# A hybrid decoder layer on one core: output weights loaded in the sixth tile, q's weights in two halves, a router that reads h, and a moved output projection

## The chip, the cores and the metric

The kernel runs on one core of a Trainium2 chip. The metric is the device time of one execution in microseconds (us), lower is better; several runs are taken and their median is compared. A core has five engines that run their own instruction streams and wait for each other on semaphores: TensorE (PE, matrix products and turns, that is transposes), VectorE (DVE), ScalarE (ACT), GpSimd (POOL), and SyncE (SP), which here only issues DMAs. All arithmetic is float32.

## What is computed

One step of a decoder layer, for a prompt of 1024 tokens (eight tiles of 128) and eight sample tokens, each with its own cache and state. The width is 1024. Cut to what matters:

```python
xn = rms_norm(x, norm1)
q, k, v, z, xbc, dt = split(xn @ w_in)
attn = sliding_window_attention(rope(norm(q)), rope(norm(k)), v, sinks)   # window 128
ssm, new_conv, new_h = ssd_mixer(z, xbc, dt, ...)     # conv of 4 taps, chunked scan, gate, norm
h = x + concat(attn, ssm) @ w_out
t = rms_norm(h, norm2)
g = softmax(t @ w_grp + b_grp);  e = t @ w_exp + b_exp        # 4 groups of 8 experts
y = h + sum over the top 2 experts of the best group: gate * (silu(t @ w_gate) * (t @ w_up)) @ w_down
```

The outputs are y for prompt and sample, and the new caches, convolution rows and states.

## The kernel before, in words

**Start.** SP issues, in this order (L364 to L396): the first tile's token rows `x`, the same rows by channel `x_chan` (a view of `mix_back`), the rope table, `norm1`, all constants `con`, the weights of q (2 MB), of k and v, of dt, eleven small parameters, two halves of xBC's weights, z's weights, the second tile's rows, and then everything that only the output stage needs: `w_out` (4 MB), `norm2`, the router's weights `w_route` and biases `b_route`. ACT squares x, POOL makes the reciprocal root, PE spreads it over the partitions (L1679), DVE scales `x_chan` into `xT` (L989). PE then projects q, k/v (`project`, L1584), xBC (`pe_xbc`, L1628) and z.

**Tile loop.** `pe_tile`, `dve_tile`, `act_tile` and `pool_tile` handle tile n and, in PE's gaps, project tile n+1. PE's order in a tile: scores (L1715), q of the next tile, products of B and C and turns (L1722, L1724), k/v and part of xBC of the next tile, turns of the probabilities (L1732), the decay product of the scan (L1737, which waits for the matrix `m`), L1739, the attention values (L1745), the state product (L1750), the rest of xBC, the turn of y (L1759, waits for the normed y), keys, z. `m` needs the cumulative sums of the tile copied to all partitions: SP writes them to memory and reads them back (`move_cum`, L405 to L410), POOL subtracts and clips (L1457, L1460), ACT exponentiates, DVE multiplies (L1067). SP's order in a tile is: rows of a later tile, `move_cum`, the spill of the mixed tile `mix` to memory (`spill`, L398).

**Output stage.** Nine turns `i`, in the order tiles 0 to 6, sample, tile 7 (`ORDER`). PE in each turn: half of the output projection (`pe_out(i, 0)`, L1644, 16 matmul records), the turn of the previous tile's t (`pe_turn_t`, L1580), the rank product of the one before (`pe_rank`), a piece of the sample's work, the other half (`pe_out(i, 1)`), the previous tile's router product (`pe_router`, L1664), more of the sample's work. A product with eight rows (`pe_state`, L1825) spreads B and C of one sample token over the partitions; ACT empties its two banks by turns (L749, L750). DVE adds the residual (`dve_residual`, L901, signal `hres`), ACT stores h and squares it, POOL makes the root (signal `hs`), DVE writes t (`dve_norm2`, L909, signal `td`), ACT stores t, PE turns it (signal `ttm`), ACT copies the turned tile to `tT`, PE multiplies with `w_route`, and DVE chooses the experts in some 20 short operations (`dve_router`, L912; `dve_rank`, `dve_choices`). `back(i)` is the buffer of x that becomes h; SP fills it and `mix_back` for turn i once turn i-2 is through (`load_next_back`, L448).

**Experts.** When the table of slots is made (`slot_table`, L1306), POOL copies the first indices (L1511), gathers rows of t (L1514) and PE runs through 32 slots of one expert each with 128 rows, whose weights SP loads four ahead; results are scattered to `y_dram`. At the end DVE adds two rows per token to h (L1407) for tiles 0 to 7 and then the sample (L1403), and ACT stores y (L840).

```python
def now(eng, names, tile):       # waits until the signal has come for this tile
    eng.wait_ge(S[name], tile + (CREDIT + 1))
def last(eng, names, tile):      # ... for the tile before
    eng.wait_ge(S[name], tile + CREDIT)
```

## Time and profile before

| | |
|---|---|
| median of 3 runs | 876.75 us (875.34 to 882.05) |
| the profiled execution | 883.72 us, of which the span of the core's instructions is 881.9 us |
| PE busy / its weight loads | 770.5 us (87%) / 548.1 us (62%) |
| DVE, ACT, POOL busy | 474.7 us (54%), 271.0 us (31%), 226.4 us (26%) |
| mean granted clock of TensorE | 0.926 of full speed |
| DMA | 140.49 MB, mean 159 GB/s |

The profile is of one execution. A row of the timeline gives the start, the duration, the engine (PEld is PE's weight load; SPq, ACTq and POOLq are queues of issues), the line, the operation, what it writes and reads, and in brackets how long the engine stood before it and what ended that. The chain of waits follows the work that ended last back to the start. The stages in the timeline: start to 53 us, tile loop to 406, output stage to 622, experts to 840, last sums to the end.

### The profile page before, as it was taken

What the parts mean: (1) busy time and instruction counts of PE and PEld (TensorE: products, weight loads), DVE (VectorE), ACT (ScalarE), POOL (GpSimd) and SP (SyncE); (2) the same over time, 40 slices, a digit from 0 to 9 for tenths busy, and PEclk for the clock granted to TensorE, in tenths of its full rate; (3) what the DMA queues carried; (4) which work ended last, traced back from release to release, by engine and by line L of the source; (5) the groups of instructions that cost most, each with busy time, mean ns of one, the idle gap of its engine ahead of it and who ended that gap; (6) DMA issues with size and microseconds to landing.
All of it is one profiled execution on the core that took longest, in us unless ns stands there. A gap on an engine that the chain in (4) does not pass through costs nothing.

```text
span 881.9 us, 12933 instructions
## 1 busy us (share of the span) xinstructions
PE 770.5 (87%) x4328; PEld 548.1 (62%) x4328; DVE 474.7 (54%) x1224; ACT 271.0 (31%) x662; POOL 226.4 (26%) x270
## 2 busy tenths in 40 slices
PE   4977999999999999986999999895799999999900
PEld 1845777776777777742564455344688877778800
DVE  1555879797979797974245443545222222222246
ACT  1342363635353636452132221201122222222200
POOL 0024233333333333230001100300334333333200
PEclk9987999999999999997998898996699999999965
DMA  7980202020202010135644551504699988886178
GB/s 257 340 223 32 98 1 86 14 98 0 97 0 96 0 51 0 48 104 177 212 169 146 188 195 67 203 3 144 218 324 331 332 308 309 296 299 250 67 263 324
DMA packets 64364, 140.49 MB, mean 159 GB/s; under 512 B 18068, under 2 KB 30132, under 8 KB 64300
## 3 DMA queue, kind: packets, MB, share of 16 engines
q1 hardware_dynamic: 51604, 110.39, 37.0%
q0 software_dynamic: 9216, 16.93, 5.2%
q10 hardware_dynamic: 3504, 12.68, 3.6%
q8 instruction: 20, 0.33, 0.2%
q14 instruction: 20, 0.16, 0.1%
HBM read 120.37 MB, written 37.34 MB: 179 GB/s over the span
## 4 chain that ended last, share of the span: by engine, by line
PE 37%; issue 20%; DMA 15%; DVE 12%; POOL 5%; POOLq 4%; DVEq 4%; ACT 2%; SPq 1%; ACTq 0%
PE bank L1644 14%; DMA w_arena<-in_w_down 9%; PE bank L1936 8%; DVE cv L1006 6%; PE bank L1942 4%; PE bank L1580 3%; DMA w_arena<-y_dram 3%; POOLq L1459 2%; PE bank L1588 2%; POOL rstd L1418 2%; DVEq L873 2%; PE bank L1628 2%; POOLq L1417 2%; POOL cv L1460 1%; DMA w_arena<-in_w_in 1%
## 5 line engine op out<-in xcount | busy, mean ns | idle before, releaser
L1644 PE MATMUL bank<-w_out_sb,mix_back 128*128 128x512 f32 x256 | 128.9, 663 | 7.0 <-issue 5.2
L1936 PEld LDWEIGHTS bank<-w_arena 128*128 128x128 f32 x992 | 116.8, 196 | 27.4 <-issue 23.2
L1936 PE MATMUL bank<-w_arena 128*128 128x128 f32 x992 | 119.8, 280 | 7.7 <-DMA w_arena<-in_w_down 6.8
L1644 PEld LDWEIGHTS bank<-w_out_sb,mix_back 128*128 128x128 f32 x256 | 53.0, 212 | 75.1 <-issue 75.0
L1588 PE MATMUL bank<-w_arena,tT 128*128 128x512 f32 (+1 forms) x192 | 73.0, 535 | 3.8 <-DMA w_arena<-in_w_in 3.8
L1588 PE MATMUL bank<-w_arena,xT 128*128 128x512 f32 (+1 forms) x192 | 72.0, 528 | 0.0
L1353 DVE TENSOR_TENSOR w_arena<-w_arena,bank 128x128 f32<-128x128 f32 x32 | 9.2, 288 | 115.0 <-ACT w_arena L805 115.0
L1006 DVE SCALAR_TENSOR_TENSOR cv<-raw,conv_w_sb,cv 128x128 f32<-128x128 f32 x192 | 65.1, 400 | 4.6 <-ACT cv L630 2.3
L1416 POOL TENSOR_TENSOR stat<-stat,eps 128x1 f32<-128x1 f32 (+4 forms) x35 | 9.1, 259 | 206.1 <-ACT junk L651 115.1
L1942 PE MATMUL bank<-w_arena 128*128 128x512 f32 x124 | 60.4, 609 | 0.7 <-DVE w_arena L1353 0.7
L1628 PEld LDWEIGHTS bank<-tT,w_arena 128*128 128x128 f32 x512 | 58.1, 192 | 1.2 <-DMA w_arena<-in_w_in 0.5
L1628 PEld LDWEIGHTS bank<-xT,w_arena 128*128 128x128 f32 x512 | 58.4, 192 | 0.5
L1628 PE MATMUL bank<-tT,w_arena 128*128 128x128 f32 x512 | 58.5, 276 | 0.1
L1628 PE MATMUL bank<-xT,w_arena 128*128 128x128 f32 x512 | 58.5, 275 | 0.0
L1588 PEld LDWEIGHTS bank<-w_arena,tT 128*128 128x128 f32 x192 | 36.3, 194 | 35.1 <-issue 33.3
L1588 PEld LDWEIGHTS bank<-w_arena,xT 128*128 128x128 f32 x192 | 35.8, 191 | 30.4 <-issue 28.6
L901 DVE TENSOR_TENSOR x<-x,bank 128x512 f32<-128x512 f32 (+1 forms) x18 | 12.4, 686 | 71.6 <-PE bank L1644 57.2
L1359 DVE COPY s<-bank 128x512 f32<-128x512 f32 x32 | 22.1, 692 | 37.0 <-PE bank L1942 37.0
L805 ACT ACTIVATE w_arena<-bank 128x128 f32<-128x128 f32 x32 | 8.9, 277 | 107.0 <-PE bank L1936 107.0
L702 ACT ACTIVATE s<-s,top 128x256 f32<-128x256 f32 x64 | 31.6, 494 | 27.9 <-DVE top L1049 27.9
L1518 POOL DMA_INDIRECT y_dram<-s,idx_out x32 | 32.5, 1015 | 24.1 <-issue 22.4
L1418 POOL TENSOR_TENSOR rstd<-stat,neg_half 128x1 f32<-128x1 f32 (+4 forms) x35 | 36.0, 1029 | 5.3 <-issue 0.6
(310 smaller groups left out, 1247.0 us busy)
## 6 DMA issues: line engine op xcount, KB each, us to landing
w_arena<-in_w_gate SPq DMA_DIRECT2D x31, 512.0 KB, 4.7
w_arena<-in_w_up SPq DMA_DIRECT2D x31, 512.0 KB, 6.2
w_arena<-in_w_down SPq DMA_DIRECT2D x31, 512.0 KB, 18.4
x<-in_x_prompt SPq DMA_DIRECT2D x16, 512.0 KB, 5.5
w_arena<-in_w_in SPq DMA_DIRECT2D x4, 2048.0 KB, 11.5
w_arena<-y_dram SPq DMA_DIRECT2D x16, 512.0 KB, 10.9
mix_back<-in_x_prompt_by_channel SPq DMA_DIRECT2D x8, 512.0 KB, 4.1
cum_rows<-cum_dram SPq DMA_DIRECT2D x8, 512.0 KB, 4.4
```

The costliest lines, as they stand in the source:

```text
L702: act.activation(s[:, hh, :], s[:, hh, :], ACT.Exp, bias=top[:, 1, hh:hh + 1], accum_out=top[:, 2, hh:hh + 1])
L873: dve.drain()
L1006: dve.scalar_tensor_tensor(out=cv[:, c, :], in0=raw[:, c, k:k + P], scalar=conv_w[:, c, k:k + 1], in1=cv[:, c, :], op0=ALU.mult, op1=ALU.add)
L1359: dve.tensor_copy(yo[u][:, 512:D], bank[7][:, :]).then_inc(E_["yd"], 1)
L1418: pool.tensor_tensor(rstd[0:n, col:col + count], stat[0:n, col:col + count], neg_half[0:n, 0:count], ALU.pow).then_inc(S[done], 1)
L1518: pool.indirect_dma_start(y_dram, bass.IndirectOffsetOnAxis(ap=idx[:, :].bitcast(U32), axis=0), out, None, bounds_check=CHOICES - 1, oob_i ...
L1580: ins = pe.transpose(bank[banks[k // 4]][:, (k % 4) * n:(k % 4 + 1) * n], cols, ids)
L1588: ins = pe.matmul(out, xT[u][:, k, 0:n], w_in[:, k, cols], start=k == 0, stop=k == KC - 1)
L1628: ins = pe.matmul(bank[half][:, c * P:(c + 1) * P], w_in[:, k, at:at + P], xT[u][:, k, :], start=k == 0, stop=k == KC - 1)
L1644: ins = pe.matmul(bank[4 - c][:, :], mix_back[u][:, k, :], w_out[:, k, 512 * c:512 * c + 512], start=k == 0, stop=k == KC - 1)
L1936: ins = pe.matmul(out[:, a * P:(a + 1) * P], gu[:, a, k, :], xgT[w % 2][:, k, :], start=k == 0, stop=k == KC - 1)
L1942: ins = pe.matmul(bank[6 + c][:, :], hidT[w % 2], down[:, 512 * c:512 * c + 512], start=True, stop=True)
```

## The change

The order of the loads at the start: x, the first 128 columns of `con`, `norm1` and `x_chan`, then q's weights in two halves by rows (signals `w_q` and `late_in`; PE waits for the second half only ahead of the fifth of eight steps), then rope and the rest of `con` (signal `w_z`). The output weights, `norm2` and the router's weights and biases are issued, in the same lines, behind the spill of tile 4, in the sixth tile. `norm2` is also loaded by channel and multiplied into `w_route` once; PE turns h instead of t, and DVE scales the router's product by the root `rstd` (two columns, 13 and 14, by turns) as it adds the bias. `load_next_back` waits for `ttm` too, since h is read longer. The first half projection of turn 0 moves into the last tile, ahead of the turn of y. The first of the two state products of turns 3, 4 and 5 moves behind the router. In the last turn the sample's router goes ahead of the second half, ACT copies the turned tile before it stores t, and DVE writes t behind the choices. The first gather takes its indices straight from the slot table. The last sums begin with the sample (`SUMS`).

```diff
+        SUMS = (TILES, *range(TILES))
@@ sync
-            token_rows(0, slice(0, P), slice(0, 1))
+            sp.sem_inc(x_in[0], 16)
+            sp.dma_start(x[0][:, :], flat_x[0:P, :]).then_inc(first_in, 16)
+            sp.dma_start(con[:, 0:P], I["constants"][:, 0:P]).then_inc(first_in, 16)
             sp.dma_start(norm1[:, :], I["norm1"].rearrange("a (p k) -> (a p) k", k=KC)).then_inc(first_in, 16)
-            sp.dma_start(con[:, :], I["constants"]).then_inc(first_in, 16)
-            weights(0, 0, Q_END, w_q)
+            sp.dma_start(x_chan[0][:, :, :], I["x_prompt_by_channel"][0]).then_inc(x_in[0], 16)
+            for half in range(2):
+                kk = slice(half * KC // 2, (half + 1) * KC // 2)
+                sp.dma_start(w_in[:, kk, 0:Q_END], w_rows[:, kk, 0:Q_END]).then_inc((w_q, late_in)[half], 16)
+            sp.dma_start(rope[0][:, :], I["rope"][0:P, :]).then_inc(x_in[0], 16)
+            sp.dma_start(con[:, P:C_END], I["constants"][:, P:C_END]).then_inc(w_z, 16)
...
             token_rows(1, slice(P, 2 * P), slice(1, 2))
-            for kv in range(NKV):
-                load(w_out[kv * HD:(kv + 1) * HD, 0:REP, :],
-                     I["w_out"][0, kv * REP * HD:(kv + 1) * REP * HD].rearrange("(r d) n -> d r n", d=HD))
-            load(w_out[:, REP:KC, :], I["w_out"][0, NH * HD:].rearrange("(c p) n -> p c n", p=P))
-            load(norm2[:, :], row("norm2", P))
-            load(w_route[:, :, 0:NG], I["w_grp"].rearrange("a (p k) n -> (a p) k n", k=KC))
-            load(w_route[:, :, NG:NG + NE], I["w_exp"].rearrange("a (p k) n -> (a p) k n", k=KC))
-            load(b_route[:, 0:NG], row("b_grp", P))
-            load(b_route[:, NG:NG + NE], row("b_exp", P))
...
             spill(4, mix_dram[4])
...
+            load(norm2_chan[:, :], I["norm2"].rearrange("a (p k) -> (a p) k", k=KC))
             rows_free(6)
...
             def load_next_back(i):
-                now(sp, "wob td", i - 2)
+                now(sp, "wob td ttm", i - 2)
...
@@ scalar
             for i in range(2, TILES + 1):
+                if i == TILES:
+                    act_router(act, TILES - 1, DEC)
                 act_residual(act, i)
+                if i == TILES:
+                    act_turned_t(act, i, width(ORDER[i]))
                 act_store_t(act, i)
-                act_router(act, i - 1, width(ORDER[i - 1]))
+                if i < TILES:
+                    act_router(act, i - 1, P)
...
@@ vector
         def dve_router(dve, tile, n, slot):
...
-            dve.tensor_tensor(lg[0:n, 0:NG], bank[7][0:n, 0:NG], b_route[0:n, 0:NG], ALU.add)
-            dve.tensor_tensor(lg[0:n, 8:8 + NE], bank[7][0:n, NG:NG + NE], b_route[0:n, NG:NG + NE], ALU.add)
+            now(dve, "hs", tile)
+            scale = rstd[0:n, 13 + tile % 2:14 + tile % 2]
+            dve.scalar_tensor_tensor(out=lg[0:n, 0:NG], in0=bank[7][0:n, 0:NG], scalar=scale, in1=b_route[0:n, 0:NG], op0=ALU.mult, op1=ALU.add)
+            dve.scalar_tensor_tensor(out=lg[0:n, 8:8 + NE], in0=bank[7][0:n, NG:NG + NE], scalar=scale, in1=b_route[0:n, NG:NG + NE],
+                                     op0=ALU.mult, op1=ALU.add)
...
             dve.wait_ge(loaded, n_loaded[0])
+            dve.tensor_tensor(w_route[:, :, :], w_route[:, :, :], norm2_chan[:, :].unsqueeze(2).to_broadcast([P, KC, NG + NE]), ALU.mult)
...
+                if i == TILES:
+                    dve_router(dve, TILES - 1, DEC, slot_of(TILES - 1))
                 dve_residual(dve, i, 1)
...
-                dve_norm2(dve, i)
+                if i < TILES:
+                    dve_norm2(dve, i)
...
             dve_choices(slice(EARLY, PAIRS), row_sel[2])
+            dve_norm2(dve, TILES)
             dve_router(dve, TILES, P, slot_of(TILES))
...
@@ gpsimd
                 last(pool, "td", tile)
-                root_mean(pool, 13, 1, n, "hs")
+                if tile >= 2:
+                    now(pool, "sel", tile - 2)
+                root_mean(pool, 13 + tile % 2, 1, n, "hs")
...
-            fetch_index(idx_in[0], 0, 0)
-            pool.drain()
-            gather(xg[0], idx_in[0], e_x[0])
+            gather(xg[0], slot_tab[:, 0, 0:1], e_x[0])
@@ tensor
-            pe_q(pe, 0, 0, P, ((w_q, 16),))
+            pe_q(pe, 0, 0, P, ((0, w_q, 16), (KC // 2, late_in, 16)))
...
                     pe_keys(nxt)
+                if n_next == DEC:
+                    pe.wait_ge(loaded, n_loaded[0])
+                    now(pe, "at", tile)
+                    pe_out(pe, 0, 0)
                 now(pe, "yg", tile)
...
         def pe_turn_t(pe, tile, n):
-            now(pe, "td", tile)
+            now(pe, "hres", tile)
             last(pe, "tt", tile)
-            pe_turn_x(pe, t[0:n, :], ident[0:n, 0:n], n, (5, 6), S["ttm"])
+            pe_turn_x(pe, back(tile)[0:n, :], ident[0:n, 0:n], n, (5, 6), S["ttm"])
```

What this makes of PE's order is shown at three places. The rows are PE's instructions in program order, with the line of the kernel they belong to (of after in the second piece; its lines are shifted), the output and inputs, the width and the number of them. `bank` is an accumulator, `con` the constants, here the identity of a turn.

The end of the tile loop and the beginning of the output stage, before:

```order
L1745 MATMUL bank<-pT,v 64x512 x4
L1750 MATMUL bank<-xde,btok 128x256 x2
L1759 MATMUL bank<-con,y 128x128 x4
L1644 MATMUL bank<-w_out_sb,mix_back 128x512 x16
L1776 MATMUL bank<-con,cum_rows 128x8 x8
```

and after:

```order
L1770 MATMUL bank<-pT,v 64x512 x4
L1775 MATMUL bank<-xde,btok 128x256 x2
L1669 MATMUL bank<-w_out_sb,mix_back 128x512 x8
L1788 MATMUL bank<-con,y 128x128 x4
L1669 MATMUL bank<-w_out_sb,mix_back 128x512 x8
L1805 MATMUL bank<-con,cum_rows 128x8 x8
```

Half of the first projection has moved ahead of the turn of y.

Turn 4 of the output stage, from its first half projection to the last piece of the sample's work, before:

```order
L1644 MATMUL bank<-w_out_sb,mix_back 128x512 x8
L1580 MATMUL bank<-con,t 128x128 x8
L1669 MATMUL bank<-both,con 128x32
L1670 MATMUL bank<-counted,con 128x32
L1825 MATMUL bank<-qT,con 128x512
L1644 MATMUL bank<-w_out_sb,mix_back 128x512 x8
L1664 MATMUL bank<-w_route,tT 128x36 x8
L1825 MATMUL bank<-qT,con 128x512
L1837 MATMUL bank<-ps_T,pT 128x8 x8
```

and after:

```order
L1669 MATMUL bank<-w_out_sb,mix_back 128x512 x8
L1604 MATMUL bank<-con,x 128x128 x8
L1694 MATMUL bank<-both,con 128x32
L1695 MATMUL bank<-counted,con 128x32
L1669 MATMUL bank<-w_out_sb,mix_back 128x512 x8
L1689 MATMUL bank<-w_route,tT 128x36 x8
L1854 MATMUL bank<-qT,con 128x512 x2
L1866 MATMUL bank<-ps_T,pT 128x8 x8
```

The state product that stood between the halves now stands with the other one behind the router, and what is turned is x, the buffer that holds h.

The last turn, from the choices on, before:

```order
L1856 MATMUL bank<-raw,s 128x32 x8
L1644 MATMUL bank<-w_out_sb,mix_back 128x512 x8
L1664 MATMUL bank<-w_route,tT 8x36 x8
L1580 MATMUL bank<-con,t 128x128 x8
L1669 MATMUL bank<-both,con 8x32
L1670 MATMUL bank<-counted,con 8x32
L1664 MATMUL bank<-w_route,tT 128x36 x8
```

and after:

```order
L1885 MATMUL bank<-raw,s 128x32 x8
L1689 MATMUL bank<-w_route,tT 8x36 x8
L1669 MATMUL bank<-w_out_sb,mix_back 128x512 x8
L1694 MATMUL bank<-both,con 8x32
L1695 MATMUL bank<-counted,con 8x32
L1604 MATMUL bank<-con,x 128x128 x8
L1689 MATMUL bank<-w_route,tT 128x36 x8
```

The sample's router went ahead of the half projection, and its rank ahead of the turn of h.

## Rows read from the trace of the kernel before

**Rows 1.** The page, its chain of waits: share of the span by engine.
```profile
PE 37%; issue 20%; DMA 15%; DVE 12%; POOL 5%; POOLq 4%; DVEq 4%; ACT 2%; SPq 1%; ACTq 0%
```
**Rows 2.** Timeline, start, PE and its weight loads (start, duration, engine, operation, wait).
```profile
13.66 12.27 PE L1588 MATMUL bank<-w_arena,tT 128*128 128x512 f32 x32 [3.84 <-DMA w_arena<-in_w_in]
25.98 14.37 PEld L1628 LDWEIGHTS bank<-tT,w_arena 128*128 128x128 f32 x128 [0.46 <-DMA w_arena<-in_w_in]
```
**Rows 3.** Timeline, first tile, SP's issues: output weights, and then the cumulative sums.
```profile
29.26 4.09 SPq L350 DMA_DIRECT2D w_out_sb<-in_w_out  x3
...
38.19 16.66 SPq L350 DMA_DIRECT2D w_route<-in_w_exp  x1
...
59.95 0.94 SPq L350 DMA_DIRECT2D b_route<-in_b_exp  x1
...
67.54 0.33 SPq L410 DMA_DIRECT2D cum_rows<-cum_dram  x1
```
**Rows 4.** Timeline, first tile: POOL's and PE's waits, and PE's next xBC.
```profile
71.07 2.44 POOL L1457 TENSOR_TENSOR cv<-cum_rows,cum 128x1024 f32<-128x1024 f32 x1 [15.45 <-DMA cum_rows<-cum_dram]
...
79.71 3.68 PE L1737 MATMUL bank<-xdt,cv 128*128 128x64 f32 x16 [5.18 <-DVE cv L1067]
...
89.67 10.88 PE L1628 MATMUL bank<-xT,w_arena 128*128 128x128 f32 x96
```
**Rows 5.** Timeline, third tile, the same two operations of PE.
```profile
171.58 1.90 PE L1737 MATMUL bank<-xdt,cv 128*128 128x64 f32 x16
...
177.16 10.88 PE L1628 MATMUL bank<-xT,w_arena 128*128 128x128 f32 x96
```
**Rows 6.** Timeline, sixth tile, two issues of SP that follow each other.
```profile
282.14 0.34 SPq L400 DMA_DIRECT2D mix_dram<-mix  x1
319.81 0.30 SPq L429 DMA_DIRECT2D x<-in_x_sample  x1
```
**Rows 7.** Timeline, last tile: PE's state products and the first output projection.
```profile
396.59 1.13 PE L1750 MATMUL bank<-xde,btok 128*128 128x256 f32 x4
...
406.79 16.98 PE L1644 MATMUL bank<-w_out_sb,mix_back 128*128 128x512 f32 x32 [5.16 <-issue]
```
**Rows 8.** Timeline, turns 3 and 4, PE.
```profile
465.50 9.79 PE L1644 MATMUL bank<-w_out_sb,mix_back 128*128 128x512 f32 x16
...
477.52 7.13 PE L1644 MATMUL bank<-w_out_sb,mix_back 128*128 128x512 f32 x16
...
499.99 1.12 PE L1825 MATMUL bank<-qT,con 8*128 8x512 f32 x2 [2.11 <-ACT kT L750]
501.04 8.83 PE L1644 MATMUL bank<-w_out_sb,mix_back 128*128 128x512 f32 x16
```
**Rows 9.** Timeline, last turn: PE, DVE's choice, POOL's first gather, PE's first expert.
```profile
600.01 1.57 PE L1580 MATMUL bank<-con,t 128*128 128x128 f32 x8 [4.31 <-DVE t L909]
...
604.26 3.60 PE L1664 MATMUL bank<-w_route,tT 128*128 128x36 f32 x16 [0.36 <-DVE rankc L950]
...
607.89 0.16 DVE L916 TENSOR_TENSOR lg<-bank,b_route 128x4 f32<-128x4 f32 x1 [1.46 <-PE bank L1664]
...
618.20 1.31 POOL L1514 DMA_INDIRECT x<-t_dram,idx_in  x1 [0.97 <-issue]
...
622.83 1.94 PE L1580 MATMUL bank<-con,x 128*128 128x128 f32 x8 [6.30 <-DMA x<-t_dram,idx_in]
```
**Rows 10.** Busy time by stretch: stretch, length, engines with counts, granted clock, DMA share, GB/s.
```profile
407.00:409.00 2.00, 2.00 (x3) 0.93 (x4) 0.00 (x0) 0.00 (x0) 0.00 (x0) 0.50 0.26 100
```
**Rows 11.** Timeline, end, the sample's sums.
```profile
877.03 2.61 DVE L1407 SCALAR_TENSOR_TENSOR x<-w_arena,gate,x 8x1024 f32<-8x1024 f32 x2
```
**Rows 12.** DMA issues: how many, KB each, median us from issue to landing.
```profile
w_arena<-in_w_down SPq DMA_DIRECT2D x31, 512.0 KB, 18.4
...
cum_rows<-cum_dram SPq DMA_DIRECT2D x8, 512.0 KB, 4.4
...
mix_back<-mix_dram SPq DMA_DIRECT2D x8, 512.0 KB, 4.8
```

More of the change, by code:

```diff
@@ L677, in _ @@
             act.sem_inc(mix_out, 16)
-            act_rows_square(act, 0, 0, 48)
+            act.wait_ge(first_in, 48)
+            last(act, "xs", 0)
+            act.activation(junk[:, :], x[0][:, :], ACT.Square, scale=D ** -0.5, accum_out=stat[:, 0:1]).then_inc(S["ssq"], 1)
             act_q(act, 0, P)
@@ L905, in dve_norm2 @@
             now(dve, "hs", i)
-            last(dve, "ttm", i)
             if i > 0:
                 dve.wait_ge(t_out, 16 * i)
-            dve.scalar_tensor_tensor(out=t[0:n, :], in0=back(i)[0:n, :], scalar=rstd[0:n, 13:14], in1=norm2[0:n, :],
+            dve.scalar_tensor_tensor(out=t[0:n, :], in0=back(i)[0:n, :], scalar=rstd[0:n, 13 + i % 2:14 + i % 2], in1=norm2[0:n, :],
                                      op0=ALU.mult, op1=ALU.mult).then_inc(S["td"], 1)
@@ L1584, in project @@
         def project(pe, u, out, n, cols, landed=()):
-            for one, count in landed:
-                pe.wait_ge(one, count)
             for k in range(KC):
+                for first, one, count in landed:
+                    if k == first:
+                        pe.wait_ge(one, count)
                 ins = pe.matmul(out, xT[u][:, k, 0:n], w_in[:, k, cols], start=k == 0, stop=k == KC - 1)
@@ L1862, in early @@
                 return row_sel[i // half], i % half
-            pe.wait_ge(loaded, n_loaded[0])
-            now(pe, "at gt", TILES - 1)
+            now(pe, "gt", TILES - 1)
             for i in range(TILES + 1):
-                if ORDER[i] < TILES:
+                if 0 < i and ORDER[i] < TILES:
                     pe_out(pe, i, 0)
-                else:
+                elif ORDER[i] == TILES:
                     last(pe, "hra hres", i)
@@ L1904, in _ @@
                 if i == 3:
+                    pe_state(2)
                     pe_state(3)
```

71 lines of the change are left out of this document (40 added, 31 removed).

## The prediction

> **What bounds the kernel now.** I read the chain of waits first: TensorE (PE) holds 37% of it, "issue" 20%, DMA 15%, VectorE (DVE) 12% [rows 1]. So no single engine sets the time, and the place of each edit has to be read by itself. I then took, place by place, the timeline of the stretch that an edit touches: the start, the first tile, the sixth tile, the change from the tile loop to the output stage, its turns, its end, and the last sums. What the reader should look for each time is the bracket behind a row, which tells how long the engine had stood and for whom, and whether the same operation is shorter elsewhere, since that tells the clock.
>
> **1. q's weights in halves, first rows ahead.** PE begins with q when all 2 MB of q's weights are there, after 3.84 us of waiting. It goes through q, k/v without a gap, and the next work, xBC, begins at 25.98, released by the landing of its own weights (0.46 us of waiting) [rows 2]. Ahead of those weights SyncE (SP) still issues the same bytes and two more DMAs, so they land when they did. Starting q earlier by up to 3.84 us therefore moves PE's wait from before q to before xBC and gains nothing: cover gone, 0. What can be lost is clock. After 5.16 us of standing, the 32 matmuls of the first output projection took 16.98 us where 16 take 7.13 elsewhere, 2.7 us too many (16.98 - 2 x 7.13) [rows 7, 8], and in the stretch of their beginning the granted clock was 0.50, which is 1.2 GHz [rows 10]. Here PE would stand at most 3.84 + 0.46 = 4.3 us, behind xBC's wait. Bounds: 0 (clock stays) and +2.7. I take **+1.8**, two thirds of the upper end, since the gap is a little shorter than that of its row.
> The Trainium skill ("TensorE: Matmul & The Clock Gate", section "HAM oscillation — how this bites in real kernels") says that matmuls that follow a wait for a DMA start at half rate, which speaks against this edit. By that rule the whole +2.7 would be paid and the sum below would be -30.4; with a clock that stays up it would be -33.1. No row of before shows a gap at this very place.
>
> **2. Output weights out of the first tile.** SP's small rows of router weights alone hold its queue for 16.66 us, and only behind them does it move the first tile's cumulative sums; their row copies are issued at 67.54 [rows 3]. GpSimd waited 15.45 us for them, PE then 5.18 us for the decay matrix, and from there to xBC's second part it took 89.67 - 79.71 = 9.96 us [rows 4] where a later tile takes 177.16 - 171.58 = 5.58 [rows 5]. With the loads gone the sums are moved as soon as they exist (48 us); with 4.4 us of landing [rows 12] and the copy to memory before it they are there by about 55, before GpSimd is free, and PE no longer waits. Late next is then PE itself, as in the later tiles. Gain 5.18 + (9.96 - 5.58) = **-9.6** (bounds: -5.2 if only the wait goes, -10 if the slow matmuls ahead of it speed up as well).
> In the sixth tile the loads stand between the spill of tile 4 at 282.14 and the sample's rows at 319.81 [rows 6], a hole of 37.7 us on SP. Before, they took SP from 29.26 to 60.9, 32 us [rows 3], part of it behind input weights; so they fit, by 6 us or more, and the seventh tile's sums are moved on time. Price 0; if the cover is gone, what rows 3 and 4 show for the first tile.
>
> **3. First out-projection ahead of the last turn of y.** In the last tile PE ends the state products at 397.7, stands until y is normed, turns y in 0.7 us, stands 5.16 us, and only then starts the projection at 406.79 [rows 7]. Its operands were loaded some 20 us before. The new order puts 7.1 us of it at 397.7; y is then turned at about 404.8, still ahead of VectorE, which is busy with the sample's q and k until 405.9. So the second half starts when the first did, at 406.8, and ends 7.1 us sooner. PE has then stood only about 1.3 us instead of 5.16, so the 2.7 us of slow clock go too: **-9.8**. Bounds -7.1 and -9.8.
>
> **4. State broadcasts of turns 3, 4, 5 behind the router.** In turns 4 and 5 PE waits 2.11 us for ScalarE (ACT) to free the bank, and the half projection behind the broadcast takes 8.83 instead of 7.13 us [rows 8], where one of the two places stands. Twice 2.11 + 1.70 is -7.6. The two broadcasts now stand together behind the router, as in turn 2, after which the next half took 9.79 us [rows 8], 0.96 more than 8.83; for turns 3 and 4 together I give back 1.9. **-5.7**; bounds -4.2 (waits alone) and -7.6. Turn 6 is bounded by VectorE's state work and stays as it is.
>
> **5. The router reads h, and the order at the end.** In turns 0 to 7 the turn of h stood behind half a projection, so nothing is gained. In the last turn PE stood 4.31 us for the norm, from 595.7 to 600.01 [rows 9]. Now the sample's router goes ahead of the last half (+0.6), so that half ends where PE now begins to stand, at 595.7 on before's time. From the same operations in the turns before I estimate: h ready 0.9 us later; turned 1.1 after that; copied by ACT, behind its square, at 599.4. The router then takes half of 3.60 (clock up) to 3.60 [rows 9]; I take 2.5: 601.9. VectorE begins the last choice 0.2 us later, at 602.1 instead of 607.89. From there to the gather were 10.31 us (618.20 [rows 9]), of which the index copy and its drain, some 1.1, go: gather at 611.3. PE began at 622.83, set by the gather's landing; it can follow only up to the table of tiles, which on VectorE ends about 5 us after the slots: 616.5. **-6.3**; bounds -3.5 (router slow, and the store of t lands last) and -8. What is late next is that store: VectorE's norm now stands behind the choices and ends at 601.2 instead of 599.95.
>
> **6. New wait on the way.** The loads of the next but one tile wait for the turn of h (ttm) as well. Behind that wait in SP's queue are first expert weights and state stores; PE waits for the tile. The turn comes about 12 us before PE needs the tile, and a load of mix_back lands in 4.8 us [rows 12]. Price 0.
>
> **7. Sample's sum first.** The sample's two sums take 2.61 us at the very end, and its store 2.3 us more to 881.9 [rows 11]. They go to where VectorE waits for loads. The last store is then 512 KB instead of 32, some 0.9 us longer: **-1.7** (-0.5 to -2.5).
>
> The expert stage keeps its length; it starts earlier. The norm's product with the router's weights on VectorE lies beside PE's projection: 0. Sum: +1.8 - 9.6 - 9.8 - 5.7 - 6.3 - 1.7 = **-31.3 us**. Against the profiled execution (883.72 us, span 881.9) that is 852.4. The median of the runs is 876.75, 7 us lower; the difference carries over, so **845.5 us**.
>
> **Rivals.**
> A. The wait moves instead of going: the sixth tile pays what the first did, because the moved loads still hold SP when the seventh tile's sums are ready. For: 32 us of SP's time before. Against: the hole of 37.7 us, in which nothing else is in the queue. Term 2 would be about 0: -21.7, **855**.
> B. The clock: PE gets less dense where products with eight rows stand together. The halves behind them take 9.79 rather than 8.83 in three turns (+2.9, of which 1.9 is in the sum: +1.0), the second half in turn 0 stays slow (+2.7), the last router takes 3.6 and its neighbours likewise (+1.6), the start pays all (+0.9), and two more halves go slow at 1.7 (+3.4). 9.6 more: **855**. For: slow halves after such products in before. Against: one fewer of them stands behind a wait.
> C. Slower: the loads of rows behind ttm land late. From the turn to the need are 12 us; six tiles (2 to 6 and 8) would each wait for (landing - 12) and start slow (2.7). It outweighs 31.3 once 6 x (landing - 12 + 2.7) is over it, a landing of about 14.5 us. Expert weights take 18.4 us to land in the expert stage [rows 12]: then 6 x (18.4 - 12 + 2.7) = 54.6, and 845.5 + 54.6 = **900**. Against: 4.8 us measured for this load, and the expert weights are issued behind it.
> D. The end gives nothing beyond its wait: the store of t, behind the h loads, sets the gather. -3.5 in place of -6.3: **848.3**.
>
> **How the numbers follow.** Forecast 0.68, A 0.09, B 0.10, C 0.04, D 0.09. A measurement of this kernel tells about 1% from no change; only C ends above 885.5, and A, B, D lie over 2% below 876.75. A mixture of several shortfalls could end within 1%; I leave it 0.03, and slower 0.04, faster 0.93. Range: all upper bounds of the gains together would be -38 (839), and A or B with a half of D 857: 839 to 857.
>
> **What would show it.** Right: GpSimd's wait of 15.45 us gone and tile one's PE row without 5.18; a gap of 3 to 4 us before the first xBC; loads of w_out between 270 and 300 and no new wait after them; the first half projection beginning right behind the state products; no 2.11 us before the broadcasts; the last turn of h within 1 us of the residual; y_prompt as the last store. Wrong: brackets of several us for mix_back before a projection (C), for cum_rows in the seventh tile (A), more than two halves over 8.8 us in turns 3 to 6 (B), the gather released by the store of t (D).

## The result, and the profile after

Before: 876.24 us, median of four runs (875.34 to 882.05). After: **852.3 us**, median of four runs (847.51 to 854.76). The ratio is 0.971, 95% interval 0.964 to 0.977. The forecast was 845.5 us and a range of 839 to 857. A second group of runs later (`c0_again` below, the same kernel) gave 847.34 us (845.37 to 855.07) against 876.35, ratio 0.968, 0.964 to 0.972. So the kernel gains 24 to 29 us by medians. Executions of one and the same program differ by up to 10 us (845.37 to 855.07), and a part of what follows is about that spread.

The profiled execution of the changed kernel took 854.76 us, span 852.8, so against the profile of before the span fell by 29.1 us. Its chain of waits, share of the span by engine, answers to [rows 1]:

```profile
PE 37%; issue 18%; DMA 14%; DVE 14%; POOL 6%; POOLq 4%; DVEq 4%; ACT 1%; SPq 1%; ACTq 0%
```

Little has moved in it: "issue" and DMA lost some, VectorE gained. That page can't say where 29 us went. Distances between the same instructions can. The table holds them, in us, for the profiles of before and after and for `c0_again`, a second profile of the changed kernel. Each stretch begins where the row above it ends.

| stretch, from one PE instruction to the next | before | after | c0_again | forecast of the change |
|---|---|---|---|---|
| span's start to the first scores | 53.30 | 56.78 | 55.47 | +1.8 |
| to the second tile's scores | 55.65 | 46.60 | 46.17 | -9.6 |
| to the last tile's state product | 287.64 | 287.70 | 287.74 | 0 |
| to turn 1's first half projection | 28.49 | 18.06 | 18.44 | -9.8 |
| to turn 2's | 20.48 | 20.48 | 20.49 | 0 |
| to turn 6's | 94.46 | 86.99 | 84.14 | -5.7 |
| to turn 8's | 35.99 | 36.60 | 35.93 | 0 |
| to the first expert | 46.82 | 43.14 | 40.65 | -6.3 |
| to the last scatter of y (GpSimd) | 217.77 | 215.79 | 214.80 | 0 |
| to the end | 41.3 | 40.66 | 39.87 | -1.7 |
| sum, the span | 881.9 | 852.8 | 843.7 | -31.3 |

**The start.** Timelines of DVE, then of PE, then SP's issues of q's weights (x2) and of the rope rows, after; they answer to [rows 2]:

```profile
13.83 1.23 DVE L1003 TENSOR_TENSOR mix_back<-mix_back,norm_sb 128x1024 f32<-128x1024 f32 x1 [9.17 <-DMA rope<-in_rope]
```
```profile
16.46 13.27 PE L1613 MATMUL bank<-w_arena,tT 128*128 128x512 f32 x32 [8.86 <-DVE tT L1006]
29.57 14.46 PE L1653 MATMUL bank<-tT,w_arena 128*128 128x128 f32 x128
...
56.78 3.78 PE L1740 MATMUL bank<-kT,qT 64*128 64x256 f32 x16 [2.67 <-issue]
```
```profile
2.65 0.98 SPq L373 DMA_DIRECT2D w_arena<-in_w_in  x2
3.67 0.93 SPq L374 DMA_DIRECT2D rope<-in_rope  x1
```

q was to begin earlier and begins 2.8 us later. VectorE scales x_chan only when its semaphore stands at 48, and that count takes in the rope rows. They were third in SP's queue; now 2 MB of weights stand ahead of 32 KB, and VectorE waits 9.17 us for rows that it does not need yet. q with k/v then took 13.27 us instead of 12.27 (12.44 in c0_again); the granted clock stands at 1.00 all through it, and no row shows why. PE's bracket names VectorE, and only VectorE's names the rope rows: a wait has to be followed by one step more. No gap stands before xBC, so no such gap can have cost clock there.

**The first tile.** Timelines of SP, POOL and PE, after, against [rows 3, 4]:

```profile
53.56 0.33 SPq L408 DMA_DIRECT2D cum_rows<-cum_dram  x1
```
```profile
59.06 2.44 POOL L1483 TENSOR_TENSOR cv<-cum_rows,cum 128x1024 f32<-128x1024 f32 x1
```
```profile
78.50 1.90 PE L1762 MATMUL bank<-xdt,cv 128*128 128x64 f32 x16
```

Both brackets, 15.45 us on POOL and 5.18 on PE, are gone, and the sixteen products take 1.90 us instead of 3.68, as in a later tile [rows 5]. The loads now stand in the sixth tile (SP, after), where [rows 6] shows the hole:

```profile
277.02 2.76 SPq L352 DMA_DIRECT2D w_out_sb<-in_w_out  x3
...
282.06 13.35 SPq L352 DMA_DIRECT2D w_route<-in_w_exp  x1
...
298.50 0.43 SPq L352 DMA_DIRECT2D b_route<-in_b_exp  x1
314.40 0.30 SPq L437 DMA_DIRECT2D x<-in_x_sample  x1
...
319.96 0.35 SPq L408 DMA_DIRECT2D cum_rows<-cum_dram  x1
```

They end at 298.9, 15.5 us ahead of the sample's rows; the seventh tile's sums are moved as always. The prediction had given this hole 6 us to spare.

**The first output projection.** PE, after, against [rows 7]:

```profile
391.08 1.13 PE L1775 MATMUL bank<-xde,btok 128*128 128x256 f32 x4
392.05 7.03 PE L1669 MATMUL bank<-w_out_sb,mix_back 128*128 128x512 f32 x16
398.92 0.60 PE L1788 MATMUL bank<-con,y 128*128 128x128 f32 x4
400.69 7.13 PE L1669 MATMUL bank<-w_out_sb,mix_back 128*128 128x512 f32 x16 [1.18 <-DVE mix L1125]
```

Two halves at 7.03 and 7.13 us instead of 16.98 for both, with 1.18 us of waiting instead of 5.16.

**Turns 3 to 5.** PE, after, against [rows 8]:

```profile
449.28 10.06 PE L1669 MATMUL bank<-w_out_sb,mix_back 128*128 128x512 f32 x16
...
471.53 8.83 PE L1669 MATMUL bank<-w_out_sb,mix_back 128*128 128x512 f32 x16
...
481.46 7.11 PE L1669 MATMUL bank<-w_out_sb,mix_back 128*128 128x512 f32 x16
...
495.01 9.37 PE L1669 MATMUL bank<-w_out_sb,mix_back 128*128 128x512 f32 x16
```

No wait of 2.11 us is left. Each turn now has one slow half, the first, where turns 4 and 5 had two. Three first halves over 8.8 us are what the prediction had named as a sign of its rival B.

**The last turn.** PE with POOL's first gather, after, against [rows 9]:

```profile
567.04 9.21 PE L1669 MATMUL bank<-w_out_sb,mix_back 128*128 128x512 f32 x16
...
577.03 1.16 PE L1604 MATMUL bank<-con,x 128*128 128x128 f32 x8 [0.47 <-DVE x L917]
...
579.57 1.98 PE L1689 MATMUL bank<-w_route,tT 128*128 128x36 f32 x16 [1.38 <-ACT tT L670]
...
591.70 1.31 POOL L1540 DMA_INDIRECT x<-t_dram,slot_tab  x1 [11.85 <-DVEq L1337]
...
596.35 1.94 PE L1604 MATMUL bank<-con,x 128*128 128x128 f32 x8 [6.01 <-DMA x<-t_dram,slot_tab]
```

PE stands 0.47 us for h instead of 4.31 for its norm, as forecast. The half ahead of it, 7.11 us before, took 9.21. Here is the same place in the second profile of the same program, and under it the granted clock, first of after and then of c0_again (columns as in [rows 10]):

```profile
561.05 7.13 PE L1669 MATMUL bank<-w_out_sb,mix_back 128*128 128x512 f32 x16
```
```profile
565.00:569.00 4.00, 4.00 (x24) 2.79 (x25) 2.86 (x13) 0.00 (x0) 0.00 (x0) 0.50 0.00 0
```
```profile
560.00:564.00 4.00, 4.00 (x28) 2.38 (x28) 3.26 (x17) 0.00 (x0) 0.00 (x0) 1.00 0.00 0
```

One execution had 0.50 (1.2 GHz) there and the other 1.00 (2.4 GHz), with PE busy all the time in both. The stretch to the first expert is 2.5 us shorter there (43.14 against 40.65), so nearly all that it lacks to the forecast is no property of the order.

### The profile page after: what moved, and what is told of

It is laid out like the page before. It is cut to its first block, busy times and chain, and to the rows that moved or that the text cites. A ratio compares the mean times of both kernels' runs of the same rounds, so it can differ in the third digit from the quotient of the medians.

```text
span 852.8 us, 12944 instructions
## 1 busy us (share of the span) xinstructions
PE 762.4 (89%) x4328; PEld 546.0 (64%) x4328; DVE 477.5 (56%) x1225; ACT 271.0 (32%) x662; POOL 225.9 (26%) x269
## 4 chain that ended last, share of the span: by engine, by line
PE 37%; issue 18%; DMA 14%; DVE 14%; POOL 6%; POOLq 4%; DVEq 4%; ACT 1%; SPq 1%; ACTq 0%
PE bank L1669 13%; DMA w_arena<-in_w_down 9%; PE bank L1962 9%; DVE cv L1023 6%; PE bank L1968 4%; PE bank L1604 3%; DMA w_arena<-y_dram 3%; PE bank L1613 2%; POOLq L1485 2%; POOL rstd L1442 2%; DVEq L889 2%; POOLq L1441 2%; POOL cv L1486 2%; PE bank L1653 2%; PE bank L1689 1%
## 5 line engine op out<-in xcount | busy, mean ns | idle before, releaser
L1669 PE MATMUL bank<-w_out_sb,mix_back 128*128 128x512 f32 x256 | 126.0, 650 | 3.0 <-DVE x L917 1.9
L1613 PEld LDWEIGHTS bank<-w_arena,tT 128*128 128x128 f32 x192 | 36.6, 195 | 40.8 <-issue 39.0
```

Source lines behind the costliest of these rows:

```text
L1613: ins = pe.matmul(out, xT[u][:, k, 0:n], w_in[:, k, cols], start=k == 0, stop=k == KC - 1)
L1669: ins = pe.matmul(bank[4 - c][:, :], mix_back[u][:, k, :], w_out[:, k, 512 * c:512 * c + 512], start=k == 0, stop=k == KC - 1)
```

## The experiments

Each kernel is the changed one with the edit shown; medians are of five or six runs. Four groups ran, on three chips, each with its own runs of before (876.35, 880.73, 876.99 and 879.27 us), so ratios are compared, and stretches of the profiles above all.

**c0_again**, no edit.

> The changed kernel once more, for a second profile and as the one that the others of this group are held against. Both theories: the time of before times 0.971 (about 851 us). Open is the slow half projection of the last turn (9.21 us, granted clock 0.50 at 565 to 569): if it is there again it belongs to the order of the instructions; if it takes 7.1 us this time, it belongs to the single execution.

847.34 us, ratio 0.968 (0.964 to 0.972). The slow half is not there again: it belonged to the single execution. So did turn 3's first half, 10.06 us in the first profile and 7.13 in this one.

**e1_rope**: the rope rows ahead of q's weights.

```
+            sp.dma_start(rope[0][:, :], I["rope"][0:P, :]).then_inc(x_in[0], 16)
             for half in range(2):
...
-            sp.dma_start(rope[0][:, :], I["rope"][0:P, :]).then_inc(x_in[0], 16)
```

> Only the issue of tile 0's rope rows goes ahead of the two halves of q's weights. Theory (a new wait: VectorE waits for a count that holds the rope rows, and these land behind 2 MB of weights, at 13.7 us): the DMA wait of 9.17 us before x_chan's scaling falls to under 3, q begins at 9 to 10.5 instead of 16.46, xBC waits some 3 to 4 us for its own weights and begins at 26 to 27.2 instead of 29.57; the time falls by 2.5 to 3.5 us. Rival (clock: the two halves of q pay for standing, whatever the rope rows do): xBC still begins at 29 or later, and the time stays.

850.61 us (845.08 to 852.87), ratio 0.969 (0.965 to 0.973). DVE, then PE:

```profile
7.12 1.23 DVE L1003 TENSOR_TENSOR mix_back<-mix_back,norm_sb 128x1024 f32<-128x1024 f32 x1 [2.45 <-DMA rope<-in_rope]
```
```profile
10.27 12.92 PE L1613 MATMUL bank<-w_arena,tT 128*128 128x512 f32 x32 [2.65 <-DMA w_arena<-in_w_in]
26.40 14.56 PE L1653 MATMUL bank<-tT,w_arena 128*128 128x128 f32 x128 [3.21 <-DMA w_arena<-in_w_in]
```

The new wait is shown: q begins 6.2 us earlier. Half of that is lost in front of xBC, which waits for its own weights, as the prediction had said of an earlier q. The first scores come at 53.72, 1.8 to 3.1 us sooner than in the two profiles of the changed kernel. The median did not follow: three runs lie at 845.1 to 848.7 us, with mean granted clocks of 0.942 to 0.946, and three at 852.6 to 852.9 us, with 0.934 to 0.936. The clock makes the two sorts; at which place it was lost is known for the profiled run alone.

**e2_rope_xbc**: as e1_rope, and xBC's first weights ahead of the small parameters.

```
+            weights(W_XBC, Z_END, Z_END + 512, w_x[0])
             for dst, src in (
...
-            for half in range(2):
-                weights(W_XBC + 512 * half, Z_END + 512 * half, Z_END + 512 * half + 512, w_x[half])
+            weights(W_XBC + 512, Z_END + 512, Z_END + 1024, w_x[1])
```

> As e1_rope, and the first 512 columns of xBC's weights are issued ahead of the eleven small parameter loads. Theory (what bounds the start then is the landing of xBC's weights, issued late behind small loads during which the DMA share is 0.2 to 0.7): q and k/v run from 9.5 to 22, xBC begins right behind them at 22 to 23.5 without a wait, 3 to 4 us ahead of e1_rope, and the first scores (56.78 in the changed kernel) come at 49 to 51; time 6 to 7.5 us under the changed kernel. Rival (the parameters are late next: ScalarE and VectorE start dt and the norms later, and PE waits for them at its cumulative sums): xBC begins early, but the scores come no earlier than in e1_rope.

**845.51 us** (843.42 to 848.03), ratio 0.964 (0.961 to 0.968). PE:

```profile
10.10 13.19 PE L1613 MATMUL bank<-w_arena,tT 128*128 128x512 f32 x32 [2.53 <-DMA w_arena<-in_w_in]
23.13 14.58 PE L1653 MATMUL bank<-tT,w_arena 128*128 128x128 f32 x128
...
50.47 3.79 PE L1740 MATMUL bank<-kT,qT 64*128 64x256 f32 x16 [2.67 <-issue]
```

xBC follows k/v with no wait, and the scores come 5.0 to 6.3 us ahead of the changed kernel's. The late parameters cost nothing: from xBC to the scores pass 27.3 us, and 27.2 in the changed kernel. What lay under the start was the queue: eleven small loads, one after the other, ahead of 2 MB that PE needs first. The median is 1.8 us under c0_again's, 6.8 under that of the first group; 6 to 7.5 were expected, and the intervals of the ratios touch.

**e3_loads_back**: the output and router weights loaded in the first tile again.

```
             token_rows(1, slice(P, 2 * P), slice(1, 2))
+            for kv in range(NKV):
+                load(w_out[kv * HD:(kv + 1) * HD, 0:REP, :],
...
             spill(4, mix_dram[4])
-            for kv in range(NKV):
-                load(w_out[kv * HD:(kv + 1) * HD, 0:REP, :],
...
```

> The output weights, norm2 and the router's weights are issued in the first tile again; all else as changed. Theory (term 2, measured between the scores and xBC's second part at 9.06 us in the two traces): GpSimd's wait of about 15 us for the cumulative sums is back, xBC's second part stands some 36 us behind the first scores instead of 27.3, and the time rises by 9 us (8 to 10). Rival A (the sixth tile had paid part of it): the time rises by less than 6, because the sixth tile gets shorter.

852.03 us, ratio 0.971 (0.967 to 0.974). SP, then PE:

```profile
68.06 0.32 SPq L418 DMA_DIRECT2D cum_rows<-cum_dram  x1
```
```profile
80.88 2.22 PE L1762 MATMUL bank<-xdt,cv 128*128 128x64 f32 x16 [2.72 <-DVE cv L1086]
```

The waits are back (12.97 us on POOL), but from the first to the second scores it took 51.09 us, 4.5 more than in the changed kernel and not 9. The median is 4.7 us over c0_again's of the same group, with intervals that overlap. The sixth tile had paid nothing: the distances from scores to scores in all later tiles are the same within 0.1 us. (In the last tile of this profile the products behind a wait of 3.45 us ran at a granted clock of 0.50, and the state product came 2.9 us later than in the changed kernel.) Neither theory foresaw the 4.5. SP reaches the sums at 68.06, where it reached them at 67.54 before [rows 3], although the scores stand 3.1 us later than before. So the end of SP's loads hardly moves with PE's start; a late start hides a part of the wait.

**e8_rope_loads** was to test that: e1_rope and e3_loads_back together.

> Two edits: the rope rows ahead of q's weights as in e1_rope, and the output weights in the first tile as in e3_loads_back. Theory (the end of SyncE's loads, and with it the cumulative sums, stands at a fixed time near 68 us; the late start hid part of it, so that the two terms don't add up): the first scores come at 53.7 as in e1_rope, the second some 54 to 55.7 us behind them (51.1 in e3_loads_back, 46.4 in e1_rope), so at 107.7 to 109.4; against e3_loads_back the time stays, within 1 to 2 us, although e1_rope takes 1.7 to 2.7 off the same place without the loads. Rival (the terms add up): the second scores at about 104.8, the time 2.7 under e3_loads_back.

855.51 us, ratio 0.973 (0.969 to 0.977). The second scores came at 110.72, but the first at 56.68 and not 53.7, so the test is spoilt. The reason is PE's xBC, here and, under it, the granted clock from 28 to 32 us in this kernel and in e1_rope:

```profile
26.49 17.42 PE L1653 MATMUL bank<-tT,w_arena 128*128 128x128 f32 x128 [2.98 <-DMA w_arena<-in_w_in]
```
```profile
28.00:32.00 4.00, 4.00 (x21) 4.00 (x21) 2.14 (x5) 0.00 (x0) 1.25 (x1) 0.50 1.05 393
```
```profile
28.00:32.00 4.00, 4.00 (x39) 4.00 (x38) 2.46 (x5) 0.00 (x0) 0.92 (x1) 1.00 1.05 392
```

Same instructions, nearly the same wait (2.98 and 3.21 us), and once the clock falls and the work takes 2.9 us more (17.42 - 14.56), once it stays. That is about the upper bound of term 1 (2.7 us). The two kernels issue the same up to xBC's weights and differ in SP's loads behind them, so that this pair alone doesn't show that chance decides. The Trainium skill ("TensorE: Matmul & The Clock Gate", section "HAM oscillation — how this bites in real kernels") has it that matmuls behind a long enough wait for a DMA start at half rate; of these two runs one shows it.

The profile shows one thing more. Its first scores stand where those of e3_loads_back do (56.68 and 56.39 us), and yet the second come 54.04 us behind them and not 51.09. SP issued the copies of the sums 1.0 us later (69.06), PE waited 4.12 us instead of 2.72, and its sixteen products behind the wait took 3.67 us instead of 2.22.

**e11_xbc_loads**: e2_rope_xbc and e3_loads_back together, since xBC has no wait there.

> The start of e2_rope_xbc and the output weights in the first tile as in e3_loads_back. e8_rope_loads was to test this, but there xBC ran slow behind its wait (granted clock 0.50 from 28 to 32 us), and the first scores came at 56.7, not 53.7. In this start xBC has no wait, so the scores should come at 50.5 to 52.4. Theory (SyncE reaches the tile's cumulative sums at a fixed time, some 67 to 69 us, whatever the start is, and the early start turns into waiting): GpSimd's copies are issued at 66 to 69, PE waits 5 to 9 us for the decay matrix, the second scores come at 105.5 to 110, and the time is that of e3_loads_back, a ratio of 0.969 to 0.973. Rival (the two terms add up): the second scores 51.1 us behind the first, at 101.6 to 103.5, and a ratio of 0.963 to 0.967.

853.15 us, ratio 0.972 (0.968 to 0.976). POOL, then PE:

```profile
68.79 2.45 POOL L1483 TENSOR_TENSOR cv<-cum_rows,cum 128x1024 f32<-128x1024 f32 x1 [14.97 <-DMA cum_rows<-cum_dram]
```
```profile
51.51 3.36 PE L1740 MATMUL bank<-kT,qT 64*128 64x256 f32 x16 [2.67 <-issue]
...
77.44 3.67 PE L1762 MATMUL bank<-xdt,cv 128*128 128x64 f32 x16 [5.53 <-DVE cv L1086]
...
106.04 2.00 PE L1740 MATMUL bank<-kT,qT 64*128 64x256 f32 x16
```

First scores 4.9 us ahead of e3_loads_back, second scores 1.4 us ahead: 3.4 of the 4.9 us turned into waiting and slow products behind it. SP issued the sums' copies at 65.36, a little sooner than expected; the ratio is in the range expected. The two terms don't add up. With the loads in the first tile an earlier start is worth little at the second scores; with them gone, e2_rope_xbc keeps it (second scores at 96.96).

The four profiles with the loads in the first tile (before, e3, e8, e11) can be put side by side. SP issued the copies at 67.54, 68.06, 69.06 and 65.36 us; from there to the second scores it took 41.4, 39.4, 41.7 and 40.7 us, while from the first scores it took 55.7, 51.1, 54.0 and 54.5. The time of the second scores follows SP more closely than PE's start. What is left goes with the clock: after waits of 5.18, 4.12 and 5.53 us (before, e8, e11) the sixteen products took 3.68, 3.67 and 3.67 us, after 2.72 us (e3) 2.22, after none 1.90.

**e4_proj_back**: the first half projection behind the turn of y again.

```
-                if n_next == DEC:
-                    pe.wait_ge(loaded, n_loaded[0])
-                    now(pe, "at", tile)
-                    pe_out(pe, 0, 0)
```

> The first half of the first output projection goes back behind the last turn of y; all else as changed. Read between the last state product and the first half of turn 1: 28.5 us before the change, 18.1 and 18.4 us in the two profiles of the changed kernel. Theory (term 3: the 7.1 us of the half are paid again in full, and the standing in front of it brings the slow matmuls back): 27 to 28.5 us, the time up by 8.5 to 10. Rival (only the half itself; the slow matmuls were chance, as the slow half of the last turn was): 25.2 to 25.6 us, the time up by 7.

860.38 us, ratio 0.979 (0.975 to 0.982). PE:

```profile
399.69 16.78 PE L1669 MATMUL bank<-w_out_sb,mix_back 128*128 128x512 f32 x32 [4.78 <-issue]
```

The stretch is 28.25 us, 9.8 to 10.2 more; the ratio is 1.1% (9 us) up. Theory shown: the 2.5 us of slow matmuls come back with the standing. In both profiles with this standing they were slow, and in none of the twelve without it.

**e5_state_back**: one state broadcast of turns 3 to 5 between the halves again.

```
+                if i == 3:
+                    pe_state(2)
...
                 if i == 3:
-                    pe_state(2)
                     pe_state(3)
```

> One of the two state broadcasts of turns 3 to 5 stands between the halves again. Read from the first half of turn 2 to that of turn 6: 94.5 us before the change, 84.1 to 87.3 us in five profiles with the changed order. Theory (term 4: two waits of 2.11 us for ScalarE, and a second slow half in each of turns 4 and 5): 92 to 95 us, both waits back, the time up by 6 to 8. Rival (clock chance alone made the difference between the traces, and a wait for ScalarE is made up later): 84 to 89.

853.86 us, ratio 0.973 (0.969 to 0.977), 0.5% or 4 us up, where 6 to 8 were expected; the intervals overlap. PE in turns 4 and 5:

```profile
482.98 1.12 PE L1854 MATMUL bank<-qT,con 8*128 8x512 f32 x2 [2.11 <-ACT kT L760]
484.03 8.83 PE L1669 MATMUL bank<-w_out_sb,mix_back 128*128 128x512 f32 x16
...
509.53 1.12 PE L1854 MATMUL bank<-qT,con 8*128 8x512 f32 x2 [2.11 <-ACT kT L760]
510.57 7.13 PE L1669 MATMUL bank<-w_out_sb,mix_back 128*128 128x512 f32 x16
```

92.32 us from turn 2 to turn 6, in the range of the theory, above all twelve profiles with the broadcasts together (82.2 to 87.4). The waits come back exactly; of the two extra slow halves one does (8.83 us), and the other takes 7.13.

**e6_router_back**: the sample's router behind the last half again, on PE, DVE and ACT.

```
                     pe_choices(range(0, half), early, chosen, stop=False)
-                    pe_router(pe, TILES - 1, DEC)
...
-                if 1 <= i < TILES:
-                    pe_router(pe, i - 1, P)
+                if 1 <= i:
+                    pe_router(pe, i - 1, width(ORDER[i - 1]))
```

> The sample's router, its choice on VectorE and its ranks stand behind the last half projection again; the norm's place and the router's reading of h stay as changed. Read from the first half of turn 8 to the first expert: 46.8 us before the change, 43.1 in the first and 40.1 to 40.7 in the other four profiles of the changed order. Theory (VectorE's chain counts: the sample's choice, 3.7 us, is put back ahead of the last tile's, where only the norm's 1.3 us and 1.3 us of gaps can be filled): 42 to 43 us with no slow half, time up by 1.5 to 2.5. Rival (the slow choices and the slow half of 9.21 us came from the router's products with eight rows ahead of the half): the half takes 7.1 us and the stretch falls to 40 or less.

850.93 us, ratio 0.969 (0.965 to 0.973): about 1 us, which these runs don't tell from none. In the profile the stretch is 42.50 us, as the theory said; the half takes 7.11, but it takes 7.13 in c0_again too.

**e7_sums_back**: `SUMS = (*range(TILES), TILES)`.

> The sample's sum goes last again, all else as changed. Read from the last scatter to the end: 41.3 us before the change, 39.4 to 40.7 us in nine profiles with the sample first. Theory (term 7): 41 to 41.8 us, the time up by 1 to 2. Rival (the end is set by how fast the loads of y come from memory, in whichever order): 40.5 or less, no change in the time that can be measured.

850.78 us, ratio 0.970 (0.966 to 0.974). The tail is 41.56 us, against 39.5 to 40.8 in all others with the sample first: 0.8 to 2.1 us. By the time alone it could not be told.

**e9_split**, and **e10_rope_xbc_split** with e2_rope_xbc's start: the router in the middle of the second half of turns 3 to 5.

```
-        def pe_out(pe, i, c):
+        def pe_out(pe, i, c, between=None):
...
+                if between and k == KC // 2:
+                    between()
...
+                split = i in (3, 4, 5)
+                if split:
+                    pe_out(pe, i, 1, lambda: pe_router(pe, i - 1, P))
```

> In turns 3, 4 and 5 the router's sixteen products with 36 columns stand in the middle of the second half projection, eight of its matmuls ahead and eight behind, and the state broadcasts alone are left between two halves; the products are the same. Theory (the halves are slow because products with few columns or few rows stand together for 3.9 to 6 us, after which the granted clock is 0.50): the first halves of turns 4, 5 and 6, now 8.6 to 8.8, 8.6 to 9.4 and 8.0 us and more, take 7.1 to 7.5 us, the stretch from turn 2 to turn 6 falls from 84.1 or more to 80 to 82, the time by 3 to 5 against the changed kernel's 0.968 of before. Rival (the clock falls by itself or after the state broadcasts alone): the halves stay at 8.6 and more, or the router's neighbours get slow in their place, and the time stays.

> The edits of e2_rope_xbc and e9_split together. If both hold: the first scores at 50.5 us, the stretch from turn 2 to turn 6 at 80 to 82, and a ratio to before of 0.959 to 0.962; if only the start's does, 0.964 as in e2_rope_xbc.

e9_split: 850.19 us, ratio 0.967 (0.962 to 0.971), turns 2 to 6 in 87.22 us. e10_rope_xbc_split: **844.20 us** (843.18 to 846.77), ratio 0.963 (0.959 to 0.967), 82.19 us. Turn 4's first half and what stands ahead of it, in e9 and then in e10:

```profile
468.81 1.98 PE L1856 MATMUL bank<-qT,con 8*128 8x512 f32 x4
470.62 0.60 PE L1862 MATMUL bank<-con,s 8*128 8x8 f32 x8
471.15 8.83 PE L1671 MATMUL bank<-w_out_sb,mix_back 128*128 128x512 f32 x16
```
```profile
460.70 1.98 PE L1856 MATMUL bank<-qT,con 8*128 8x512 f32 x4
462.52 0.60 PE L1862 MATMUL bank<-con,s 8*128 8x8 f32 x8
463.06 7.13 PE L1671 MATMUL bank<-w_out_sb,mix_back 128*128 128x512 f32 x16
```

The same instructions with the same gaps, 8.83 us in one and 7.13 in the other. Turn 6's first half took 7.0 us in both, against 8.0 to 8.8 in most others, but it took 7.0 in e5_state_back and e11_xbc_loads too, which don't split. The expectation of e9 fell. Of e10's, the stretch and nearly the ratio were met (0.963 against 0.959 to 0.962), but not the start: the first scores came at 52.39 and not at 50.5, since the second half of xBC's weights was late:

```profile
32.22 7.41 PE L1653 MATMUL bank<-tT,w_arena 128*128 128x128 f32 x64 [1.39 <-DMA w_arena<-in_w_in]
```

So the three profiles with e2_rope_xbc's start have their first scores at 50.47, 51.51 and 52.39 us, against 55.3 to 56.8 in the eight with the changed kernel's. Whether splitting is worth anything stays open. e2_rope_xbc and e10_rope_xbc_split are the fastest versions. They are faster than the kernel before beyond doubt. Against the changed one they gain 2 to 8 us of medians, with intervals that still overlap.

## Why the prediction was right, and where it was not

**Term 1, q in halves: +1.8 forecast, +3.5 and +2.2 measured, by another cause.** The step that failed is "Starting q earlier by up to 3.84 us": the list of what q's start waits for (x_chan's count, which takes in the rope rows) was not held against the new order of SP's queue. The diff shows both lines. VectorE's wait of 9.17 us, 8.68 in c0_again, came in the place of the gap that was forecast ahead of xBC. That an earlier q gains little of itself (cover by xBC's weights) was right: e1_rope gets 3.21 us of waiting there. The clock cost, its only price in the text, did not arise: there was no gap ahead of xBC, and the granted clock was 1.00 from 8 to 40 us in both profiles. That the number has the right sign is luck.

**Term 2, the loads: -9.6 forecast, -9.1 and -9.5 measured.** Right in size and cause. What the text did not see is that terms 1 and 2 are tied (e3, e8, e11): had the loads stayed, 4.5 us would have been the price at this late start, and one 4.9 us earlier would have kept 1.4 us of it. Rival A is refuted: no tile pays.

**Term 3, the projection: -9.8 forecast, -10.4 and -10.1 measured**, and -9.8 to -10.2 undone by e4_proj_back. Right in all its parts, the 1.3 us of remaining wait (1.18, and 1.56 in c0_again) too.

**Term 4, the broadcasts: -5.7 forecast, -7.5 and -10.3 measured**, -5.0 to -10.1 by e5_state_back, against the twelve others. The waits (4.2) were exact. The slow halves were mis-sized: the text gave back 1.9 us for pairs, where most profiles show 8.5 to 9.4 us in turns 4 and 5, one slow half for two. Turn 3's is 7.1 us in five profiles and 8.6 to 10.1 in eight, and the same program shows both.

**Term 5, the end: -6.3 forecast, -3.7 and -6.2 measured**, -5.9 to -6.7 in the ten other profiles with this order. In the profiled execution the step "that half ends where PE now begins to stand" failed: choices, router and half took 0.7, 0.4 and 2.1 us more at 0.50. One item was wrong in every run: from the last choice to the gather were 10.31 us and are 10.12 (591.70 - 581.58), so dropping the index copy gave 0.2, not 1.1. From the last write of the slots to the gather's issue were 1.26 us with the copy and its drain between (616.94 to 618.20) and are 0.95 without (590.75 to 591.70). Rival D did not happen: the gather's bracket names VectorE's slots.

**Term 6: 0, as forecast.** No PE row before a projection has a bracket for mix_back; its loads land in a median of 3.8 us after. Rival C is refuted.

**Term 7: -1.7 forecast, -0.6 and -1.4 measured**, -0.8 to -2.1 by e7_sums_back.

**The expert stage** was to keep its length and took 2.0 and 3.0 us less; but it spreads over 214.2 to 217.4 us in the thirteen profiles, and nothing in the change acts there. It is left as spread, its cause not shown.

**The sum.** It was -31.3 against -29.1, and that it is so close is in part luck: in the first profile term 4 gave 1.8 us more than forecast and term 5 2.6 less, term 1 cost 1.7 more, and 2.0 us came from the expert stage, which no edit touches.

**The median.** Of the 6.8 us between 845.5 and 852.3 the sum is 2.2. The rest comes from the step "the difference carries over": the profiled execution of before lay 7.0 us above its median of 876.75, that of after 2.5 above its own, and 4.5 us of what was subtracted is that difference. The clock goes with it. The profiled execution's mean granted clock was 0.926; of the eleven runs of before beside c0_again, three have 0.924 to 0.926 and took 879.7 to 880.9 us, and eight have 0.932 to 0.935 and took 873.3 to 876.9.

**Rival B** was no separate case but a part of many runs. By its sign, more than two halves over 8.8 us in turns 3 to 6, the first profile meets it (10.06, 8.83, 9.37) and c0_again does not (none over 8.7); but before has five such halves, so the sign could not tell B from the kernel as it was. Its other places, the second half in turn 0 and the start, stayed fast in both. In most groups the longer runs have the lower mean clock (c0_again: 845.37 us at 0.946, 855.07 at 0.939), but not in all pairs (849.79 at 0.939 too), so the clock is shown as a large part of the 10 us and not as all of it.

## What to carry to other kernels

When a load is put ahead of others, list every semaphore count that the consumer waits for, and everything that feeds it; one small load behind 2 MB made an edit meant to start earlier start later, and moving it back with the next weights ahead of small loads was worth 3 to 6 us at the first scores. A wait that is set by the end of a queue's own work hides what is late before it and swallows most of what is early, so that such terms must be worked out together. Where one execution of a program differs from the next by 1%, two profiles are compared stretch by stretch, and a gain read from one is not taken from the median until it is known in which part of the spread that profile lay.

## What the runs showed that was not expected

The granted clock does not follow from the program alone: one program took 9.21 us and 7.13 for the last half (after, c0_again), and 10.06 and 7.13 for turn 3's first. Two more pairs, of kernels that differ elsewhere, show the same with the waits equal within 0.3 us: 17.42 against 14.56 for xBC (e8, e1) and 8.83 against 7.13 for turn 4's half (e9, e10). Slow stretches stand behind a wait or behind products with few columns or rows, but at many such places only in a part of the executions. After the longer standing of about 5 us ahead of the first projection they were there both times.

The rope rows, 32 KB, were issued at 3.67 us and VectorE was released at 13.83, 10.2 us later, while the DMA engines moved a mean of 389 GB/s from 8 to 14 us. In e1_rope they were issued at 2.65, ahead of q's weights, and it was released at 7.12, 4.5 us later. Here the small transfer came in behind the 2 MB that stood ahead of it. The Trainium skill ("DMA: Bandwidth & Descriptors", section "Queues, rings and completion order") says that each DMA engine consumes the descriptors of a ring in order, though they need not complete in order, and that one issuing engine has one ring on each; the rows agree with the first.
